# A two-block transformer on one core: six modulation pieces moved from TensorE to VectorE, their totals taken behind the attention

## What is computed

```python
c_act = silu(c)                                   # one row of 1024
sh1, sc1, g1, sh2, sc2, g2 = split(c_act @ w_mod[0] + b_mod[0], 6)
h = rmsnorm(x, a_norm_g) * (1 + sc1) + sh1
mix = forgetting_attention(h, a_w_in, a_b_f, a_w_o)   # q, k, v, forget logits = h @ a_w_in
x = x + g1 * mix
h = rmsnorm(x, ffn_norm_g) * (1 + sc2) + sh2
x = x + g2 * grouped_moe(h, ...)
```

## Time and profile before

| | before |
|---|---|
| median of 3 runs | 1947.54 us (1942.72 to 1950.5) |
| the profiled execution | 1946.94 us, its span 1945.2 us |
| PE busy | 1679.4 us, 86% of the span |
| DVE busy | 1071.5 us, 55% |
| ACT busy | 622.5 us, 32% |
| POOL busy | 271.7 us, 14% |
| read from memory | 607.89 MB, 313 GB/s over the span |
| DVE busy from 60 to 130 us | 25.8 us of 70 |

### The profile page before, as it was taken

How to read it: one execution, slowest core, us unless ns; L and a number is a source line. 1 busy time by engine, 2 the same in 40 slices (tenths; PEclk the granted TensorE clock), 3 DMA queues, 4 the chain that set the end, 5 groups by cost and what they waited for, 6 DMA issues and landing times.

```text
span 1945.2 us, 24570 instructions
## 1 busy us (share of the span) xinstructions
PE 1679.4 (86%) x9499; PEld 824.3 (42%) x9499; DVE 1071.5 (55%) x2220; ACT 622.5 (32%) x1092; POOL 271.7 (14%) x315
## 2 busy tenths in 40 slices
PE   4998899988989899999998998989787777688786
PEld 1866632222356574333335454683333333233232
DVE  4337723232474663224139993378666666766654
ACT  1336333433234633544422023143222222122221
POOL 0000100000000000000200000025333333343330
PEclk9999999999989999999998999999989999899989
DMA  9881499999947418999981334369999999999995
GB/s 355 292 303 44 154 393 408 409 409 409 359 166 248 174 44 347 400 398 393 404 310 45 122 130 141 114 269 423 425 425 425 425 424 425 424 425 425 425 425 225
DMA packets 154452, 610.55 MB, mean 314 GB/s; under 512 B 14280, under 2 KB 16496, under 8 KB 120800
## 3 DMA queue, kind: packets, MB, share of 16 engines
q1 hardware_dynamic: 114336, 325.98, 44.0%
q0 software_dynamic: 39296, 280.11, 34.7%
q10 hardware_dynamic: 704, 2.90, 0.4%
HBM read 607.89 MB, written 1.05 MB: 313 GB/s over the span
## 4 chain that ended last, share of the span: by engine, by line
PE 54%; DMA 28%; DVE 13%; ACT 2%; issue 2%; SPq 0%; DVEq 0%; ACTq 0%
PE PS L1013 15%; DMA peer_rows<-in_peer_rows,MOD 15%; PE PS L998 8%; PE PS L1307 8%; DMA AR<-in_peer_rows,MOD 6%; PE PS L767 5%; PE PS L758 4%; PE PS L788 2%; DMA peer_rows<-in_down_units 2%; DVE AR L1666 2%; DMA peer_rows<-in_exp_w_up 2%; DMA ring<-in_w_mod 2%; DMA MOD<-in_peer_rows,MOD 1%; PE PS L1255 1%; PE PS L811 1%
## 5 line engine op out<-in xcount | busy, mean ns | idle before, releaser
L1307 PE MATMUL PS<-peer_rows,HT 128*128 128x512 f32 x724 | 356.4, 645 | 99.2 <-ACT HT L1652 99.2
L2484 DVE SCALAR_TENSOR_TENSOR peer_rows<-peer_rows,PS 128x1024 f32<-128x1024 f32 x181 | 220.7, 1219 | 136.0 <-DMA peer_rows<-in_peer_rows,MOD 134.6
L1013 PE MATMUL PS<-peer_rows,AR 128*32 128x512 f32 (+1 forms) x1920 | 289.1, 592 | 0.1
L1307 PEld LDWEIGHTS PS<-peer_rows,HT 128*128 128x128 f32 x724 | 145.9, 206 | 305.5 <-issue 177.6
L2078 DVE COPY MOD<-peer_rows 128x1024 f32 x96 | 66.5, 694 | 294.9 <-PE PS L1013 97.6
L1013 PE MATMUL PS<-MOD,AR 128*32 128x512 f32 x640 | 225.9, 592 | 0.0
L717 POOL DMA_INDIRECT peer_rows<-in_peer_rows,MOD x181 | 171.0, 945 | 309.0 <-PE PS L1307 250.9
L998 PE MATMUL PS<-peer_rows,AR 128*32 128x512 f32 x1280 | 155.7, 605 | 10.7 <-DMA peer_rows<-in_down_units 5.7
L1013 PEld LDWEIGHTS PS<-peer_rows,AR 128*32 128x32 f32 x1920 | 78.6, 110 | 193.8 <-issue 185.8
L1430 ACT ACTIVATE MOD<-peer_rows 128x1024 f32 x96 | 96.1, 1049 | 142.8 <-DMA peer_rows<-in_down_units 54.3
L1307 PE MATMUL PS<-AR,HT 128*128 128x512 f32 x240 | 117.5, 630 | 25.1 <-ACT HT L1652 25.1
(11 more groups left out here) (406 smaller groups left out, 2611.8 us busy)
## 6 DMA issues: line engine op xcount, KB each, us to landing
peer_rows<-in_exp_w_gate SPq DMA_DIRECT2D x128, 512.0 KB, 8.8
peer_rows<-in_exp_w_up SPq DMA_DIRECT2D x128, 512.0 KB, 7.6
peer_rows<-in_down_units SPq DMA_DIRECT2D x128, 512.0 KB, 8.7
ring<-in_w_mod SPq DMA_DIRECT2D x20, 2048.0 KB, 9.3
ring<-in_w_in SPq DMA_DIRECT2D x7, 2048.0 KB, 8.8
ring<-in_a_w_in SPq DMA_DIRECT2D x6, 2048.0 KB, 11.7
peer_rows<-in_kv_w_mod SPq DMA_DIRECT2D x16, 512.0 KB, 9.9
peer_rows<-in_w_mod SPq DMA_DIRECT2D x16, 512.0 KB, 10.2
```

Source lines behind the costliest of these rows:

```text
L1013: last = [nc.tensor.matmul(PS[QUARTER * i:QUARTER * i + QUARTER, banks + tile, :], left[:, tile, at + k, QUARTER * i:QUARTER * i + QUARTER ...
L1307: last = nc.tensor.matmul(PS[:, 4 + 2 * c + half, :], diagonal(k), v_row(k)[:, 512 * half:512 * half + 512], start=j == 0, stop=j == SEL - 1)
L2484: V.scalar_tensor_tensor(u_row(k), u_row(k), 1.0, PS[:, 2 * c:2 * c + 2, :].rearrange("p a k -> p (a k)"), ALU.mult, ALU.mult, accum_out=D ...
```

## The change

The six `mod0_b` pieces get a kind of their own, "V". DVE multiplies each of the slab's eight blocks (128 x 512) by one column of `cT` and adds it to `MOD` (`add_slab`), 48 chained operations, each waiting for the one ahead. The slab is released by the eighth of them (`mod_added`) instead of by `mod_partial`. `add_slab(0)`, `(1)`, `(2)` stand in DVE's order behind the low parts of units 3, 7 and 11; `(3)` behind unit 18, `(4)` behind unit 22, `(5)` behind the forget gates and ahead of the attention's first mask. `MOD[:, 2 * D:5 * D]` starts as zeros with the bias in partition 0 alone: a memset on POOL at the start and one transfer of 12 KB. The broadcast that stays is 1024 columns. The partials, totals, ACT copies and DVE adds of the six pieces are gone from the projections. Behind the attention's last values and ahead of `a_o`, PE sums the six 128 x 512 pieces of `MOD` over partitions with `ones` (banks 4 and 5 in turn), and ACT copies each total back into `MOD` in all partitions; piece i waits for the copy of piece i-2. DVE waits for the six copies ahead of the low parts of `a_o` from the fourth on.

```diff
@@ -210,10 +210,11 @@
                 if kind == "M":
                     mod_no[len(pieces)] = len(mod_no)
                 pieces.append(name)
-                n_done[0] += kind != "M"
+                n_done[0] += kind not in "MV"
                 done_at.append(n_done[0])
             slabs.append(dict(src=w[:, c0:c0 + n].rearrange("(b p) n -> p b n", p=P), kb=kb, n=n,
-                              release=("mod_partial", len(mod_no)) if kind == "M" else ("gemm_done", n_done[0]),
+                              release=("mod_partial", len(mod_no)) if kind == "M" else
+                              ("mod_added", pieces.count(name)) if kind == "V" else ("gemm_done", n_done[0]),
                               pieces=n_done[0]))
 
     def stream_cut(name, w, kb, cols, kind="N"):
@@ -256,7 +257,7 @@
     MOD0 = {"mod0_a": 0, "mod0_b": 2 * D, "mod0_d": 5 * D}
 
     def stream_mod0(name, first, n):
-        stream(name, A["w_mod"][0], DB, cols(512 * n, at=MOD0[name] + 512 * first), "M")
+        stream(name, A["w_mod"][0], DB, cols(512 * n, at=MOD0[name] + 512 * first), "V" if name == "mod0_b" else "M")
 
     SCALE_FIRST = (2, 3, 0, 1)
     for part in SCALE_FIRST:
@@ -305,6 +306,9 @@
     evac_by = {name: "v" for name in (*MOD0, *MOD1, "a_o", "b_o", "attn_up", "c_o")}
     evac_at, n_by = [], {"v": 0, "a": 0}
     for g, name in enumerate(pieces):
+        if name == "mod0_b":
+            evac_at.append(None)
+            continue
         e = evac_by.get(name, "a")
         n_by[e] += 1
         evac_at.append(("evac_" + e, n_by[e]))
@@ -315,15 +319,13 @@
         pair_of[g] = 4 + 2 * i
     for i, (g, *_) in enumerate(stages["a_qk"] + stages["a_v"]):
         pair_of[g] = 2 * (i % 2)
-    for g, *_ in stages["mod0_b"]:
-        pair_of[g] = 4
     for i, (g, *_) in enumerate(stages["c_o"]):
         pair_of[g] = 2 * i
     for g, *_ in stages["peer_q0"]:
         pair_of[g] = 0
     for i, (g, *_) in enumerate(stages["peer_q"]):
         pair_of[g] = 2 * (i % 2 == 0)
-    before = [max((h for h in range(g) if pair_of[h] == pair_of[g]), default=None) for g in range(len(pieces))]
+    before = [max((h for h in range(g) if pair_of[h] == pair_of[g] and pieces[h] != "mod0_b"), default=None) for g in range(len(pieces))]
 
     def slab_view(r, kb, n):
         return ring[:, (r % RING) * SLAB:(r % RING) * SLAB + kb * n].rearrange("p (b n) -> p b n", n=n)
@@ -653,12 +655,14 @@
             bcast(GAIN[:, 0:src.shape[0]], src, "gain_in")
 
         load_gain("a")
+        link(pool, pool.memset(MOD[:, 2 * D:5 * D], 0.0), "pool")
+        pool.dma_start(MOD[0:1, 2 * D:5 * D], A["b_mod"][0, 2 * D:5 * D].rearrange("(a n) -> a n", a=1)).then_inc(S("modb0_in"), 16)
         bcast(bf[:, :], A["a_b_f"][0], "small_in")
         bcast(rb[:, :], A["router_bias"], "small_in")
         pool.dma_start(rw[:, :, :], A["router_w"].rearrange("(b p) n -> p b n", p=P)).then_inc(S("small_in"), 16)
         pool.dma_start(pos_i[:, :], A["positions"][0].rearrange("(c p) -> p c", p=P)).then_inc(S("small_in"), 16)
         pool.wait_ge(S("gemm_done"), 1)
-        bcast(MOD[:, 2 * D:], A["b_mod"][0, 2 * D:], "modb0_in")
+        bcast(MOD[:, 5 * D:], A["b_mod"][0, 5 * D:], "modb0_in")
         load_gain("ffn0")
         pool.wait_ge(S("slots"), 1)
         for g in range(MOD_GROUPS):
@@ -1085,16 +1089,8 @@
         tp("h_a", per_chunk=("h_ready", h_no["a"]), only=slice(0, 1))
         mod_total(*stages["mod0_a"][3])
         tp("h_a", per_chunk=("h_ready", h_no["a"]), only=slice(1, 4))
-        beside = stages["mod0_b"]
-        for i in range(4):
-            gemm("a_qk", None, only=slice(i, i + 1))
-            if i:
-                mod_total(*beside[i - 1])
-            mod_partial(*beside[i])
-        for i in range(2):
-            gemm("a_v", HT, only=slice(2 * i, 2 + i))
-            mod_total(*beside[3 + i])
-            mod_partial(*beside[4 + i])
+        gemm("a_qk", None)
+        gemm("a_v", HT)
 
         pe.wait_ge(S("logf"), 1)
         for c in range(C):
@@ -1103,9 +1099,14 @@
                 last = nc.tensor.matmul(PS[:, 7, HEADS * c:HEADS * c + HEADS], ones, F[:, 0, :],
                                         start=False, stop=True)
         last.then_inc(S("early_mm"), 1)
-        mod_total(*beside[5])
-        tp("cum", ("negcum", 1), evac_at[beside[5][0]])
+        tp("cum", ("negcum", 1))
         attention("A", [ht("cum"), evac_at[stages["a_v"][-1][0]]])
+        pe.wait_ge(S("mod_added"), len(stages["mod0_b"]))
+        for i, (_, _, _, n, _) in enumerate(stages["mod0_b"]):
+            if i >= 2:
+                pe.wait_ge(S("mod_summed"), i - 1)
+            at = MOD0["mod0_b"] + 512 * i
+            nc.tensor.matmul(PS[:, 4 + i % 2, 0:n], ones, MOD[:, at:at + n], start=True, stop=True).then_inc(S("mod_sum"), 1)
         gemm("a_o", None)
         gemm_mod("mod0_d")
         experts(0)
@@ -1490,7 +1491,7 @@
         def qk_out(i, banks):
             dst = (z["Q"] if i < 2 else z["K"])[:, 4 * (i % 2):4 * (i % 2) + 4, :]
             return A_(dst.rearrange("p (u a) t -> p u (a t)", u=2), banks, ACT.Copy, scale=0.125 if i < 2 else 1.0)
-        evac("a_qk", qk_out, after="a_v", beside=lambda i: mod_copies("mod0_b", slice(i, i + 1)))
+        evac("a_qk", qk_out, after="a_v")
 
         def v_out(i, banks):
             if i == 0:
@@ -1501,13 +1502,17 @@
                 act.wait_ge(S("f_log"), 1)
                 A_(Ft, Ft, ACT.Ln, bias=ones[:, 0:1]).then_inc(S("f_log"), 1)
             return to_rows(z["V"])(i - 1, banks)
-        evac("a_v", v_out, beside=lambda i: i and mod_copies("mod0_b", slice(3 + i, 4 + i)))
+        evac("a_v", v_out)
         act.wait_ge(S("early_mm"), 2)
         cum = PS[:, 7, 0:C * HEADS].rearrange("p (c h) -> p c h", c=C)
         A_(Fn[:, :, 0:HEADS], cum, ACT.Copy, scale=-1.0)
         A_(Fn[:, :, 64:64 + HEADS], cum, ACT.Copy, scale=-1.0).then_inc(S("negcum"), 1)
         tp("cum")
         attention("A", out="a_o")
+        for i, (_, _, _, n, _) in enumerate(stages["mod0_b"]):
+            act.wait_ge(S("mod_sum"), i + 1)
+            at = MOD0["mod0_b"] + 512 * i
+            A_(MOD[:, at:at + n], PS[:, 4 + i % 2, 0:n], ACT.Copy).then_inc(S("mod_summed"), 1)
         highs("a_o", STAGES)
         mod_copies("mod0_d", slice(0, 1))
         square("a_o")
@@ -2186,12 +2191,29 @@
             V.tensor_tensor(low, value, high.bitcast(fp32), ALU.subtract).then_inc(S("lhs_cut"), 1)
             lows("a_qk", half, half + 1)
         lows("a_qk", 2, STAGES)
-        lows("a_qk", STAGES, 11)
         wait("modb0_in", 16)
-        add_mod0("mod0_b", slice(0, 1))
-        lows("a_qk", 11, 15)
-        add_mod0("mod0_b", slice(1, 2))
-        lows("a_qk", 15)
+        wait("c_ready", 2)
+
+        def add_slab(i, only=range(DB)):
+
+            _, r, _, n, _ = stages["mod0_b"][i]
+            wait(f"slab{r % RING}", 16 * (r // RING + 1))
+            at = MOD0["mod0_b"] + 512 * i
+            for k in only:
+                last = V.scalar_tensor_tensor(MOD[:, at:at + n], slab_view(r, DB, n)[:, k, :], cT[:, k:k + 1], MOD[:, at:at + n],
+                                              ALU.mult, ALU.add)
+                if k == DB - 1:
+                    last.then_inc(S("mod_added"), 1)
+                else:
+                    L(last)
+
+        lows("a_qk", STAGES, 4)
+        add_slab(0)
+        lows("a_qk", 4, 8)
+        add_slab(1)
+        lows("a_qk", 8, 12)
+        add_slab(2)
+        lows("a_qk", 12)
 
         wait("small_in", 64)
         wait("consts_in", 32)
@@ -2203,7 +2225,7 @@
         reduce_angle(RA, RB_)
         dve.sem_inc(S("ang"), 1)
         lows("a_v", 0, STAGES)
-        add_mod0("mod0_b", slice(2, 3))
+        add_slab(3)
         lows("a_v", STAGES, STAGES + 1)
 
         wait(*evac_at[stages["a_v"][0][0]])
@@ -2211,13 +2233,15 @@
         V.scalar_tensor_tensor(Ft, F, -1.0, F, ALU.mult, ALU.max).then_inc(S("f_abs"), 1)
         ts(F, F, 0.0, ALU.min)
         lows("a_v", STAGES + 1, STAGES + 4)
-        add_mod0("mod0_b", slice(3, 4))
+        add_slab(4)
         lows("a_v", STAGES + 4)
         wait("f_log", 2)
         V.tensor_tensor(F, F, Ft, ALU.subtract).then_inc(S("logf"), 1)
-        add_mod0("mod0_b", slice(4, 6))
+        add_slab(5)
         attention("A", out="a_o")
         cut_lhs("a_o", "o", 7, 8)
+        wait("mod_summed", len(stages["mod0_b"]))
+        wait("modb0_in", 32)
         lows("a_o", STAGES)
         scale_gain("ffn0", mod_part(4))
         add_product("a_o", mod_part(2))
```

## The result

The changed kernel takes 1953.03 us (median of 22 runs, 1948.54 to 1957.23) against 1949.09 us (22 runs, 1941.52 to 1954.87) of the kernel before on the same chips. The ratio is 1.0022, 95% interval 1.0014 to 1.0030: slower by 4.3 us, 2.7 to 5.8. The forecast was 6.0 us slower, 1953.5. That the absolute time is met to 0.5 us is luck: the forecast started from a median of 3 runs that lies 1.55 us under the one of 22, and was 1.7 us too large in the difference. The prediction also held that under 0.5% nothing could be told from no change; with 22 runs on each side the interval is 0.08% either way, and 0.22% stands clear of it. The profiled execution took 1954.34 us with a span of 1952.5 us.

What follows compares the result with a forecast made beforehand. PE was taken to bound the projections, with slab landings right behind. 1.8 us at the mask plus 4.2 behind the attention gave 6.0: 1952.9 profiled, 1953.5 us median; bounds 1950 to 1959, eight in ten 1946 to 1960.

Steps and rivals of the forecast that it cites:

- A piece costs 6.3 us on DVE: Projections: eight chained multiply-add steps of 0.79 us take 6.3 us of DVE per slab, bounds 5.8 to 6.6.
- Three waits for low parts: Ahead of units 4, 8 and 12 PE idles some 1.3 us each for low parts delayed by DVE's adds.
- r13 issued 5.5 us earlier: End of a_qk: low part 15 frees the slot at 91.45, so r13 is issued then, against 96.98 before.
- r14 issued late: In a_v: the slot is released only after `add_slab(3)`, so r14 is issued at 110.2 instead of 105.88.
- r15 lands 14.9 behind r14's issue: In a_v: slab r15 lands at 125.1, 14.9 us after r14's issue as before; bounds 13.5 to 19.4.
- PE stands 13.3 us: In a_v, before unit 20: PE idles from 114.25 for 13.3 us; unit 20 starts at 127.6, 4.3 later.
- Its cost there is covered by the fifth add: Units 20 to 22: a slow clock after idling costs up to 1.7 us, hidden behind `add_slab(4)`.
- The mask 1.8 later: Start of the attention: the first mask starts at 143.8, 1.8 us later than before.
- Totals 5.2, net 4.2: Behind the attention: six totals take 5.2 us of PE, partly in an existing wait, so 4.2 us later.
- The sum, 6.0: Whole kernel: 1.8 us at the mask plus 4.2 behind the attention make it 6.0 us slower.
- The rival that PE's time is saved: Projections: work taken off PE gains 14.4 us at the attention, less 4.2 behind it: -10.2, 1937.3 us; chance 0.06.
- The rival of the slabs slipping: Projections: r8 lands no earlier, giving +9.7, 1957.2 us, or 1961.7 with late r15; chance 0.18 together with a slow clock.

Runs made afterwards that it cites:

- the added-products run: Changed kernel with the fourth add moved ahead of three low parts, plus 13 idle PE products between forget logits and unit 16: 1946.81 us, ratio 0.9982.

## Why the prediction was right

- *A piece costs 6.3 us on DVE*: 6.26. All 48 steps, the view of one line:

```profile
L2203 DVE SCALAR_TENSOR_TENSOR MOD<-ring,cT,MOD x48: 743/752/753, 53.6 to 143.9; 128x512 f32<-128x512 f32 x48
```

The row of the same operation elsewhere had 748. The formula of the Trainium skill ("VectorE: DVE Perf Modes", errata section) would have given an estimate of 0.59 us; the measurement decides, and the page's own warning for single operations holds. The prediction's "some 3 us less" by that figure was added up too small: four adds lie on the way to r14, each 1.2 us shorter by it, which makes 4 to 5. Nothing else used it.
- *Three waits for low parts*: forecast near 1.3 each, measured 1.29, 1.24 and 1.19. r8 landed at 71.70, 28.3 behind the token cut (27.7 forecast), in time for DVE.
- *r13 issued 5.5 us earlier*: 49.2 behind the cut, 48.9 forecast. It took 9.2 us to land where I had taken 7.8: this term was 1.4 too small. It repeats: r13 took 7.8 to 8.0 us in the four executions with the partials on PE, and 8.9 to 9.4 in the nine with the adds on DVE. In the changed kernel's trace r13's transfer runs at 300 to 450 GB/s until 99.4, much as before, and then falls to 8 to 31 GB/s for most of 2 us until the last bytes are there; in the kernel before that tail is missing. What makes it stays open.
- *r14 issued late*: 69.2 behind the cut, 67.7 forecast, the difference being r13. *r15 lands 14.9 behind r14's issue*: 13.8, too large by 1.1. Before, r15 was issued 3.7 behind r14, now at once; the two errors add up to 0.3. That unit 20 came out where it was forecast is luck in this: neither landing was right by itself.
- *PE stands 13.3 us*: 9.2. Units 16 to 19 took 13.94 us instead of 11.0, at a granted clock of 0.50 in their first 4 us and 0.60 in the next 2. Of the 4.1 us by which the stand is shorter, 2.9 are this clock and 1.6 the later start of unit 16 behind r13; 0.4 go the other way, as unit 20 starts that much later than forecast. That cost nothing, since PE waited for r15 anyhow. I had looked for the slow clock only behind the long wait. *Its cost there is covered by the fifth add*: units 20 to 23 took 12.67, 12.45 forecast.
- *The mask 1.8 later*: 2.1. *Both ways end together*: DVE waited 0.32 for the scores.
- *Totals 5.2, net 4.2*: 5.54 and 4.17. Leaving them out shows 4.20.
- *The sum, 6.0*: 6.3 in the first pair of profiles from token cut to multiply, 7.9 in the second. The timed ratio says 4.3, 2.7 to 5.8, which just leaves out 6.0 and both pairs. So the mechanism is shown stretch by stretch, and its net size is not settled: two executions of the changed kernel differ by 1.4 us in the projections and by 6.1 in the rest, and some 2 us stay open.

The rival that PE's time is saved needed r15 11 us earlier. Moving one line gave it that (r15 lands 71.0 behind the token cut instead of 83.0), and the sign turned: 3.3 us faster than the kernel before by the ratio of 0.9983, 3.1 in the trace up to the multiply. It is a third of the rival's 10.2. The rest is time in which PE stood or ran slowly all the same: 3.3 us ahead of unit 16, for r13 and what ACT does behind it; 1.8 in units 16 to 19 by the clock (12.82 instead of 11.0); and 1.6 ahead of unit 23, whose low part stands in DVE's order behind the fifth add. There the next limit of this version lies. The rival of the slabs slipping did not come: r8 was in time. The rule that activity releases the clock (the Trainium skill, "TensorE: Matmul & The Clock Gate", section "What's actually happening") agreed in kind behind the long wait: 0.50 from 128.8 to 131, back at 1.00 by 133. It cost the changed kernel nothing there, as the fifth add covered it. It doesn't cover the fall in the added-products run, where PE was busy throughout; there the measurement decides.

## What to carry to other kernels

Work that ends with the release of a buffer has two prices: its own time, and the delay of all that waits for the buffer behind it in the transfer queue. When such work moves to another engine, place it in that engine's order by the release, ahead of anything that waits for a later slab. Read "engine X is busy throughout" together with the landing times of what X works on next: time taken off X is worth only as much as the next landing moves.

## What the runs showed that I had not expected

- TensorE's granted clock fell during or right behind the narrow products (128x16) of the forget logits, with no idle time ahead. The windows of the kernel after, from the forget logits on:

```profile
97.00:102.50 5.50, 5.50 (x46) 5.50 (x45) 0.00 (x0) 0.69 (x1) 0.00 (x0) 0.90 0.53 198
102.50:105.70 3.20, 0.48 (x3) 0.37 (x2) 2.80 (x3) 3.17 (x4) 0.00 (x0) 0.50 0.00 0
105.70:108.00 2.30, 2.27 (x5) 1.82 (x6) 2.23 (x4) 0.00 (x0) 0.00 (x0) 0.50 0.00 0
...
112.00:119.70 7.70, 7.66 (x34) 5.99 (x32) 2.09 (x5) 0.46 (x2) 0.00 (x0) 1.00 0.76 272
...
128.80:131.00 2.20, 2.11 (x5) 1.77 (x6) 2.20 (x3) 0.56 (x1) 0.00 (x0) 0.50 0.83 306
```

0.50 is 1.2 GHz, 1.00 is 2.4. In the first window PE is busy for all of its 5.50 us and the clock has already come down (0.90 in the mean), ahead of the wait for r13. In the run with the smaller bias transfer the units follow the narrow products at once and the clock is 0.62 all the same; in the run with r14 held back it is 1.00 up to 109.0, 0.65 in the next microsecond and 0.50 from 110 to 112, inside unit 16, again with PE busy throughout; and with 13 products of 128 columns put in between it stays at 0.50. In both executions of the kernel before, the same narrow products were followed by 1.00. So they don't always bring it down, and what decides stays open. It is worth 1.6 to 3 us on four units.
- Of two slabs issued together the second landed 13.2 to 13.8 us behind the first one's issue; 3.7 us apart it was 14.5 to 14.9.
- Two executions of the changed kernel differ by 6.1 us in the part behind the first multiply, and two runs of the same projections by 3.4 us. That sets how small an effect can be read from a single profile.
